# The order of the adding transfer and the long weight sums on GpSimd, in the up projections of a Hymba layer

## The reference, cut to what matters

```
h = modulate(rms_norm(x, ffn_norm), shift, scale)
x = x + 0.5 * gate * ((silu(h @ w1) * (h @ w3)) @ w2)
```

## Time and profile before

| what | value |
|---|---|
| median of 3 runs | 1018.17 us (1016.67 to 1020.95) |
| the profiled execution, its own time | 1020.35 us |
| its span on the core | 1018.6 us |
| PE busy | 991.1 us (97%) |
| DVE busy | 751.4 us (74%) |
| ACT busy | 502.9 us (49%) |
| POOL busy | 225.7 us (22%) |
| granted clock of TensorE, mean | 0.997 |

### The profile page before, as it was taken

The page is one execution under the profiler, slowest core; times in us unless marked ns, Lnnn a source line. Parts: engine busy times, 40 slices in busy tenths (PEclk is TensorE's granted clock), DMA queues, the critical chain, the costliest instruction groups (busy, mean ns, idle before and its releaser), DMA issues.

```text
span 1018.6 us, 18633 instructions
## 1 busy us (share of the span) xinstructions
PE 991.1 (97%) x6974; PEld 862.8 (85%) x6974; DVE 751.4 (74%) x1039; ACT 502.9 (49%) x690; POOL 225.7 (22%) x191
## 2 busy tenths in 40 slices
PE   7999999999999999999999989999999999999997
PEld 5779999999888888776677767878999999988887
DVE  5777777887787858879899995566877877683334
ACT  5545444444333124588977973465444444433221
POOL 0023444453112301100100000202444443200100
PEclk9999999999999999999999999999999999999999
DMA  9556657665788736622221202235677676552322
GB/s 351 213 174 155 197 149 212 167 195 152 270 289 311 280 134 218 215 98 73 74 84 42 83 23 77 90 120 138 173 211 189 180 205 167 186 179 90 103 83 83
DMA packets 64470, 163.79 MB, mean 161 GB/s; under 512 B 5696, under 2 KB 8016, under 8 KB 64416
## 3 DMA queue, kind: packets, MB, share of 16 engines
q1 hardware_dynamic: 44720, 110.79, 30.6%
q0 software_dynamic: 18416, 50.16, 19.9%
q10 hardware_dynamic: 1280, 2.10, 0.9%
HBM read 158.83 MB, written 2.10 MB: 158 GB/s over the span
## 4 chain that ended last, share of the span: by engine, by line
PE 81%; DMA 5%; ACT 5%; DVE 5%; issue 2%; SPq 1%; DVEq 0%; POOLq 0%; ACTq 0%
PE psum L1907 15%; PE psum L1909 15%; PE psum L1908 14%; PE psum L1979 10%; PE psum L1981 10%; PE psum L1980 10%; DMA sraw_a<-ws 4%; DMA raw<-wu 1%; PE psum L2284 1%; PE psum L2278 1%; ACT whi L589 1%; PE psum L2208 1%; DVE wlo L1377 1%; PE psum L2210 1%; PE psum L2209 1%
## 5 line engine op out<-in xcount | busy, mean ns | idle before, releaser
L589 ACT ACTIVATE whi<-raw 128x1024 fp32r<-128x1024 f32 x92 | 97.3, 1057 | 221.1 <-PE psum L1909 209.5
L1125 DVE TENSOR_TENSOR wlo<-raw,whi 128x1024 fp32r<-128x1024 f32 x94 | 118.1, 1256 | 117.3 <-ACT whi L589 116.9
L1909 PE MATMUL psum<-ghi,wlo 128*128 128x512 f32 (+2 forms) x384 | 144.0, 375 | 0.0
L1908 PE MATMUL psum<-glo,whi 128*128 128x512 f32 (+2 forms) x384 | 143.3, 373 | 0.0
L1907 PE MATMUL psum<-ghi,whi 128*128 128x512 f32 (+2 forms) x384 | 143.2, 373 | 0.0
L1907 PE MATMUL psum<-hhi,whi 128*128 128x512 f32 x320 | 129.2, 404 | 2.0 <-DVE wlo L1125 1.3
L1909 PE MATMUL psum<-hhi,wlo 128*128 128x512 f32 x320 | 125.2, 391 | 0.0
L1908 PE MATMUL psum<-hlo,whi 128*128 128x512 f32 x320 | 125.0, 391 | 0.0
L1979 PE MATMUL psum<-forms,whi 128*128 128x256 f32 x432 | 121.2, 281 | 0.0
L1980 PE MATMUL psum<-forms,whi 128*128 128x256 f32 x432 | 120.7, 279 | 0.0
L1981 PE MATMUL psum<-forms,wlo 128*128 128x256 f32 x432 | 120.7, 279 | 0.0
(11 more groups left out here) (272 smaller groups left out, 2344.7 us busy)
## 6 DMA issues: line engine op xcount, KB each, us to landing
raw<-wu SPq DMA_DIRECT2D x96, 512.0 KB, 3.4
ada<-wada POOLq DMA_DIRECT2D x56, 512.0 KB, 5.1
sraw_a<-ws SPq DMA_DIRECT2D x36, 512.0 KB, 5.9
raw<-ws SPq DMA_DIRECT2D x36, 512.0 KB, 6.0
sraw_b<-ws SPq DMA_DIRECT2D x36, 256.0 KB, 4.3
sraw_a<-ws POOLq DMA_DIRECT2D x18, 512.0 KB, 6.1
raw<-ws POOLq DMA_DIRECT2D x18, 512.0 KB, 6.0
early<-wada SPq DMA_DIRECT2D x16, 512.0 KB, 15.3
```

Source lines behind the costliest of these rows:

```text
L589: nc.scalar.activation(whi[:, slot, :], raw[:, slot, :], ACT.Copy).then_inc(hi_done, 1)
L1125: nc.vector.tensor_tensor(wlo[:, slot, :], raw[:, slot, :], whi[:, slot, :], ALU.subtract).then_inc(lo_done, 1)
L1908: nc.tensor.matmul(dst, a, rlo, start=False, stop=False)
L1909: return nc.tensor.matmul(dst, b, rhi, start=False, stop=stop)
```

## The change

On POOL, in `up_sums`, the adding transfer of group g + 1 is issued ahead of the long sums of group g. Before, it came right behind them. No instruction is added or taken away, and no other engine's program changes.

```diff
                 j0 = PAIRS * n
                 add_fourth(j0, 0)
+                add_fourth(j0, 1)
                 long_sums(j0, 0)
-                add_fourth(j0, 1)
                 with pool.Fori(j0, j0 + PAIRS - 1) as j:
+                    add_fourth(j + 1, 0)
                     long_sums(j, 1)
-                    add_fourth(j + 1, 0)
+                    add_fourth(j + 1, 1)
                     long_sums(j + 1, 0)
-                    add_fourth(j + 1, 1)
                 long_sums(j0 + PAIRS - 1, 1)
```

## The result

The changed kernel takes 1038.01 us (median of 4 runs, 1036.61 to 1041.49) against 1017.85 us for the kernel before (median of 4, 1016.67 to 1020.95), run beside it: a ratio of 1.0205, 95% interval 1.0184 to 1.0227, some 20 us slower. The direction and the first of two loops were forecast; the size was forecast as 8 us. The profiled execution took 1036.61 us by its own time with a span of 1034.9 us, 16.3 us over the profiled one of before; it is the fastest of the four runs, while that of before is among the slower ones of its kernel, so that the profiles show 16 of the 20 us. What follows is counted against the 16.3.

A forecast was written before the change was run, and what follows sets the result against it. PE, busy 97% of the span, was the bound, with about 4 us to win. A 10.27 us loop against PE's 9.86 gave +2.2 and +5.8 us in the up projections: 1020.35 + 8 = 1028.3 us; 8-in-10 range 1014 to 1052 us.

The forecast's parts named there:

- the first of two loops: Adding issue, first sum, DVE's part 1, base pair, next adding issue: 10.27 us per group against PE's 9.86.
- The distance of 3.95 us: In the loop, from the adding issue to the base pair's issue on SP: forecast as 4.0 us.
- The landing: Base pair's second load, from its issue to landing: 4.96 us, taken between two earlier rows of 5.1 and 4.4 us.
- rival 1: Loop stays under PE's 9.86 us, the 3.9 us of waits go: about 1014 us; chance 0.18 including no effect.
- the term of 0.09 us: Added to the loop: DVE's late part 0 of even groups holds the next first sum some 0.2 us every second group.
- the costs that I set to nothing: First group's delayed first sum, later second sums about 5 us behind the issue, and the wait on POOL: priced at nothing.
- Rival 2: POOL's second sum runs before DVE's part 1: loop 11.0 us, +32 us over the forecast, 1050 us; chance 0.26.
- the tail behind the last adding issue: From group 17's adding issue to the up projection's end: 4.0 us, five products of 1.41 us, 9.86 us; together 20.9 us.

The follow-up runs named there:

- e9: Changed kernel with DVE's last combinations of the group before run ahead of the low half of the long sums; 1022.29 us, ratio 1.0025.
- e5: Changed kernel with DVE's wait for the first sum moved to SP, and POOL's long sums waiting for both low halves of their group; 1039.32 us, 1.0206.
- e6: Kernel before, with only the even groups' adding transfers issued ahead of the long sums of the odd group before; 1026.22 us, ratio 1.0078.
- e7: Kernel before, with only the odd groups' adding transfers issued ahead of the long sums of the even group before; 1026.21 us, ratio 1.0074.
- e3: Changed kernel with the next group's adding transfer issued between the first and second long sum; 1018.20 us, ratio 1.0005.
- e10: Changed kernel with the first-sum wait moved from DVE to SP and DVE's last combinations ahead of the sums' low half; 1026.18 us, ratio 1.0062.

## Why the prediction was wrong in size

**What held.** The loop is the one that was written down, link by link: issue and first sum end 2.51 us behind the start of the issue (forecast 2.56), DVE starts 0.04 us later, SP 0.2 us behind the low half (130.28 + 1.22 = 131.50 to 131.68). The distance of 3.95 us was forecast as 4.0. The start of the loop did not move (85.08 us against 85.34 in the earlier trace rows). The ends are later in both up projections, and the delay is carried to the end.

**The landing was a little too dear.** I took 4.96 us for the second load, between the earlier trace rows. In the loops of the first form it was 4.0 to 5.1 us, 4.5 us on average; for the pair of 131.68 us the time from issue to landing of the two loads:

```profile
DMA to landing us min/median/max: 3.4/4.2/5.0
```

With this the first form takes 9.72 us on average against a forecast of 10.18. Had all loops been of this form, the loop would have stayed under PE's pace, which is rival 1's condition; e9 comes close to it (26 of 30 loops) and still did not win rival 1's 4 us. That the price of the landing was too high hid part of the loss that the prediction had missed: 0.46 us too much there against 0.73 us in the other forms, where 0.09 us had been put. That the mean loop came out near the forecast, 10.45 for 10.27 us, is luck.

The prediction also set the Trainium skill's fit beside it ("DMA: Bandwidth & Descriptors", Anatomy of one DMA): an estimate of 4.4 us for the pair from its first issue. That section is about transfers that GpSimd issues, and this pair is issued by SP. Measured from the first issue, the pair took 4.6 to 5.7 us in the first form.

**The step that failed is the term of 0.09 us.** I wrote that DVE's part 0 of an even group comes late, by the row of upper parts, combinations and SiLU, and would hold the next first sum for 0.2 us in every second group. It is the other way round: the adding issue and the first sum stand back to back now, and a part 0 that starts 0.28 us or more behind the issue is shut out until the sum is over. That costs the base pair 2.0 us, in 10 of 30 loops, not 0.2 us in 15. These loops take 1.78 us more than those of the first form, 17.8 us together, and the 4 loops of the second form 4.2 us: the 22 us that make 9.72 into 10.45. Nor was it only even groups behind SiLU; in 7 of the 10 it was an odd group's part 0, behind gating on DVE. I had followed the path that makes part 0 late, and had not closed it: behind part 0 come part 1, the base pair and the adding issue two groups on, which is a second loop. The chain of the changed kernel shows one turn:

```profile
200.62 1.75 POOL xs L514
202.45 2.35 POOL xs L517
204.83 1.07 ACT hix L720
...
207.06 0.68 DVE csum L1400
...
208.93 0.95 DVE g L1412
209.87 2.03 DVE wlo L1377
...
212.82 2.31 DVE wlo L1377
215.29 0.37 SPq L454
215.86 4.29 DMA raw<-ws
```

From the adding issue of 199.84 to that of 220.79 it is 20.95 us for two groups, 1.2 us over PE's pace. The two low halves take 5.3 us of it, 3.0 us more than where nothing shuts them out (2.36 us, the rows of e5 below); without that the turn would be some 18 us (an estimate that leaves the landing as it is), under PE's pace. Late and shut out go together here. It was also among the costs that I set to nothing: "there is room for it while the loop sets the pace" was said of the second sums for PE's products 4 and 5, and it was true for PE (it waits 14.0 us for `wlo`, and the low halves of the sums are not among its longer waits); I did not ask it for what stands behind them on DVE and ACT. E9 shows that this loop carries most of the loss: shortened, it leaves no distance of 6.0 us, and the 16 to 18 us that come back are what those ten loops had cost. E6 and e7 show that it doesn't need the first one; what takes it over PE's pace is the shut-out here and the slower landing in e6.

**Rival 2** was priced about right (5.2 us of distance for 5.15, 11.0 us for 10.77) but came in 4 of 30 loops, in the first ones. It was not an either-or, as I had set it up.

**In the sum:** mean loop 10.45 for 10.27 us, 30 x 0.18 = 5.5 us; the tail behind the last adding issue 22.4 us (241.44 to 263.9) and 22.5 us for 20.9, together 3.1 us. In the first tail POOL's sums shut out the last low half of the group before (1.08 us for 0.68) and gating (1.71 for 0.95) and so made the last group's part 0 late by 1.2 us. 8.0 + 5.5 + 3.1 - 0.3 for the earlier start is the 16.3 us of the profiles.

**Left open.** The 4 us between the two profiled executions and the medians are not explained: which form a loop takes hangs on a few hundredths to tenths of a us, and executions of the changed kernel spread over 5 us. The trace is of one execution.

**The issue alone does not shut DVE out.** Part 0 started 0.28 to 1.05 us behind the issue, up to 0.5 us ahead of the sum's stamp, and waited all the same, so the issue itself could be blamed. In e5 no sum can run right behind the issue, since it waits for the low halves:

```profile
724.27 1.20 POOL L508 DMA_DIRECT2D sraw_a<-ws  x1 [4.07 <-DMA sraw_a<-ws]
724.49 2.36 DVE L1376 TENSOR_TENSOR wlo<-raw,whi 128x1024 fp32r<-128x1024 f32 x2 [1.33 <-ACT whi L721]
727.03 1.28 POOL L515 TENSOR_TENSOR xs<-raw 128x512 f32<-128x512 f32 x1 [1.55 <-DVE wlo L1376]
```

The two low halves start 0.22 us behind the issue and take 2.36 us, 1.22 us each, as if alone; the same holds up to 1.35 us behind it. It takes the sum right behind the issue to shut them out. Why DVE then has to wait from before the sum's stamp stays open.

## What to carry to other kernels

Before an issue is moved ahead of work, write down every path from the moved work back to the issue, not only the shortest, and over two turns of the buffers as well as one; the engines' program order counts as a link like any semaphore. Price each loop against the pace of the engine that is the bound: here loops of 9.8 us on average (e9) held PE up only in the first groups, and 10.45 us cost 0.6 us in each of 30 groups. When a loop that has transfers in it is shortened, look at the distance between their issues; the link taken out may have been what kept them apart.

## What the hardware showed that I had not expected

- A low half on DVE (two inputs in SBUF) that starts 0.28 to 1.05 us behind an adding issue of POOL (1.20 us) with a sum right behind it waits for the end of that sum: 2.59 to 3.31 us in place of 1.22. In e3 one that started 0.19 us behind took 3.43 us. At 0.16 and 0.17 us behind the issue it ran in 1.23 and 1.22 us. With no sum right behind the issue it ran undisturbed (e5, 0.22 us behind: 1.22 us).
- When one instruction's end releases DVE and POOL at once, the stamps differ by 0.02 to 0.05 us, and the earlier one went first in all 20 such loops of the changed kernel, DVE in 16 and POOL in 4, and in all 30 of e9, 26 and 4.
- A pair of loads of 0.5 MB each: the second lands in 4.0 to 5.1 us when the adding transfer was issued 3.95 us ahead of the pair (changed kernel), in 5.3 to 7.6 us when it was 2.6 us (e10), and in 6.4 to 7.7 us when it was 1.3 us (kernel before).
